# One stage instead of two: a layer's input products and its linear attention in a transformer kernel

## The reference, cut to what matters

```python
z = split_columns((rmsnorm(x, pre_g) * (1 + scale) + shift) @ w_in)
# pool branch: windowed means, a 128x128 product per group, a gate
y_pool = einsum('blgi,gio->blgo', multiscale_pool(z['pool_x']), pool_w) * pool_scale * silu(z['pool_gate'])
# GLA: decays, then a scan over chunks of 64 tokens, forwards and backwards
log_a = log_sigmoid(z['gla_af'] @ af_w2 + af_b) / 16        # and the same for gla_ab
y_gla = rmsnorm(scan_f + flip(scan_b), g) * silu(z['gla_gate'])
merged = sum(sigmoid(z['merge_b']) * (y_b @ w_branch_b) for b in (mla, pool, gla))   # 3 x 8 tiles of 128 columns
x = x + gate * rmsnorm(merged @ w_out, post_g)
```

## Time and profile before

| what | us |
|---|---|
| median of 3 runs | 1573.66 (1570.69 to 1574.66) |
| profiled execution | 1576.58 |
| its span in the trace | 1574.8 |
| PE busy in it | 1392.7 (88%) |
| mean granted TensorE clock | 0.946 of full speed |

### The profile page before, as it was taken

How to read it: one execution, slowest core, us unless ns; L and a number is a source line. 1 busy time by engine, 2 the same in 40 slices (tenths; PEclk the granted TensorE clock), 3 DMA queues, 4 the chain that set the end, 5 groups by cost and what they waited for, 6 DMA issues and landing times.

```text
span 1574.8 us, 24551 instructions
## 1 busy us (share of the span) xinstructions
PE 1392.7 (88%) x10288; PEld 1164.0 (74%) x10288; DVE 860.0 (55%) x1213; ACT 637.9 (41%) x1002; POOL 730.3 (46%) x512
## 2 busy tenths in 40 slices
PE   5898899999999999688889699979799888799996
PEld 1654588677777787373777689968688777799996
DVE  1566605351333340756687565659889635488811
ACT  2445332342322323446424464556422123565542
POOL 0520044323213554050494866747745204499983
PEclk8899999999999999899999899989899999999998
DMA  8320033244335432130333333525222123355552
GB/s 342 109 67 14 28 94 100 66 148 170 106 114 207 142 100 80 32 115 14 109 118 104 112 107 122 167 85 179 94 82 82 55 83 114 96 179 186 185 177 80
DMA packets 48830, 179.73 MB, mean 114 GB/s; under 512 B 5457, under 2 KB 6481, under 8 KB 48337
## 3 DMA queue, kind: packets, MB, share of 16 engines
q1 hardware_dynamic: 48576, 176.08, 34.3%
q10 hardware_dynamic: 144, 2.10, 0.3%
HBM read 177.11 MB, written 1.05 MB: 113 GB/s over the span
## 4 chain that ended last, share of the span: by engine, by line
PE 62%; DVE 22%; ACT 7%; DMA 3%; POOL 3%; issue 3%; ACTq 0%; DVEq 0%; SPq 0%
PE ps L367 16%; PE ps L371 15%; PE ps L368 15%; PE ps L369 15%; DMA panels<-weights 3%; DVE work L1776 2%; POOL panels_r L411 1%; POOL panels_r L412 1%; ACT panels_hi L401 1%; PE ps L879 1%; DVE work L1220 1%; DVE small L926 1%; DMA const_sb<-constants 1%; DVE work L1174 1%; DVE work L988 1%
## 5 line engine op out<-in xcount | busy, mean ns | idle before, releaser
L411 POOL TENSOR_TENSOR panels_r<-panels,panels_hi 128x512 fp32r<-128x512 f32 x254 | 368.5, 1451 | 823.5 <-ACT panels_hi L401 822.1
L368 PE MATMUL ps<-h_sb_r,panels_hi 128*128 128x256 f32 (+1 forms) x1408 | 455.3, 323 | 0.0
L401 ACT ACTIVATE panels_hi<-panels 128x1024 fp32r<-128x1024 f32 x254 | 267.2, 1056 | 420.6 <-PE ps L369 251.2
L412 POOL TENSOR_TENSOR panels_r<-panels,panels_hi 128x512 fp32r<-128x512 f32 x254 | 375.0, 1476 | 0.0
L367 PE MATMUL ps<-hi_sb_r,panels_hi 128*128 128x512 f32 (+1 forms) x784 | 280.3, 358 | 32.9 <-DVE h_sb_r L613 14.0
L368 PEld LDWEIGHTS ps<-h_sb_r,panels_hi 128*128 128x128 f32 x1408 | 278.4, 198 | 18.4 <-issue 1.2
L369 PE MATMUL ps<-hi_sb_r,panels_r 128*128 128x512 f32 (+1 forms) x784 | 274.6, 350 | 0.0
L367 PEld LDWEIGHTS ps<-hi_sb_r,panels_hi 128*128 128x128 f32 x784 | 154.8, 197 | 58.6 <-DVE h_sb_r L613 15.3
L367 PE MATMUL ps<-h_sb_r,panels_hi 128*128 128x256 f32 x624 | 184.6, 296 | 12.3 <-DVE h_sb_r L594 7.6
L367 PE MATMUL ps<-work_r,panels_hi 128*128 128x256 f32 (+1 forms) x560 | 183.1, 327 | 11.5 <-POOL panels_r L412 7.4
L369 PE MATMUL ps<-h_sb_r,panels_r 128*128 128x256 f32 x624 | 180.4, 289 | 0.0
(11 more groups left out here) (321 smaller groups left out, 1825.1 us busy)
## 6 DMA issues: line engine op xcount, KB each, us to landing
panels<-weights SPq DMA_DIRECT2D x326, 512.0 KB, 3.5
x_sb<-x_in SPq DMA_DIRECT2D x1, 2048.0 KB, 8.3
x_sb<-x_in ACTq DMA_DIRECT2D x1, 2048.0 KB, 8.7
const_sb<-constants SPq DMA_DIRECT2D x1, 1216.0 KB, 10.8
out<-x_sb SPq DMA_DIRECT2D x2, 512.0 KB, 2.9
vec_sb<-vectors SPq DMA_DIRECT2D x1, 725.0 KB, 12.1
small<-c_in SPq DMA_DIRECT2D x1, 8.0 KB, 1.6
```

The lines of the kernel that those rows point to most:

```text
L368: pe.matmul(o, lhsT.hi, rhs.lo, start=False, stop=False)
L401: act.activation(panels_hi[:, m:m + PANEL * P], panels[:, n:n + PANEL * P], ACT.Copy).then_inc(panel_rounded, 1)
L411: pool.tensor_tensor(panels_r[:, at:at + half], panels[:, at:at + half], panels_hi[:, m:m + half], ALU.subtract)
L412: pool.tensor_tensor(panels_r[:, at + half:at + 2 * half], panels[:, at + half:at + 2 * half], panels_hi[:, m + half:m + 2 * half], ALU.su ...
```

## The change

The two stages become one. The decay products now stand behind the tiles and in front of the values, in banks 4 to 7, so that none waits for a bank; ACT's absolute values and DVE's minima follow there, the minima into an area of their own (`la_first`). The values move to banks 1, 2, 3, 0 and the pool mixing behind them to banks 2, 0, 1, 3, so that the merge items can follow at once in banks 4 to 7. ACT's exponential and logarithm come behind the values, and DVE mixes items 0 and 1 between its scans (layer 1; item 0 in layer 0). In layer 1 step 2 of the table moves to an earlier place, behind tile 3, and each later step but the last one place forward; step 6 stands behind the minima. The four decay blocks move in the stream: they no longer share a panel with the pool blocks, so each layer has one panel more (328 for 326), which is the one in front of the values.

```diff
+        add(f"gla_w{l}", ...)          # now in front of gla_v, was behind pool_w
...
-   ("vector", 1): s5_factors, ("vector", 3): s5_turns(0, 2), ("vector", 9): s5_turns(2, 3),
-   ("vector", 10): s5_turns(3, 4), ("vector", 11): s5_turns(4, 5)} if last else {})
-            inputs = stages.pop()
+   ("vector", 1): s5_factors, ("vector", 3): s5_turns(0, 3), ("vector", 9): s5_turns(3, 4),
+   ("vector", 10): s5_turns(4, 5), ("vector", 11): s5_turns(5, 6)} if last else {})
+            head = stages.pop()
+            v_banks, mix_banks = (1, 2, 3, 0), (2, 0, 1, 3)
...
+            def pool_products(pe):
+                for g in range(4):
+                    pe.wait_ge(windowed, wd0 + g + 1)
+                    if g < 2:
+                        pe.wait_ge(v_act, va0 + g + 1)
+                    else:
+                        pe.wait_ge(v_dve, vd0 + g - 1)
+                    blocks.product(pe, ps[:, mix_banks[g], 0:TQ], blocks.lhs(pe, plan[f"pool_w{l}"] + g),
+                                   pooled[:, g, :, :].rearrange("p s t -> p (s t)"), True, True, mix_filled)
...
+            def decay_banks_free(pe):
+                pe.wait_ge(*by_dve)
+                pe.wait_ge(by_act[0], by_act[1] - 1)
...
-            stages.append(Stage(inputs_tensor, inputs_scalar, inputs_vector, None))
...
             def items(pe, first, end):
                     if i >= 2:
                         pe.wait_ge(mixed, m0 + i - 1)
+                    else:
+                        pe.wait_ge(w_min, wm0 + 2 * i + 2)
...
             def decay_products(pe):
+                inputs.decay_banks_free(pe)
                 for i in range(4):
-                    if i == 3:
-                        pe.wait_ge(w_min, wm0 + 1)
-                    blocks.product(pe, ps[:, i % 3, 0:TOK], ...)
+                    blocks.product(pe, ps[:, 4 + i, 0:TOK], ...)
...
             def decay_vector(dve):
-                for i in range(4):
-                    dve.wait_ge(w_abs, wa0 + i + 1)
-                    dve.tensor_scalar(la[...], ps[:, i % 3, 0:TOK], decay_bias(i), 0.0, ALU.add, ALU.min)...
                 dve.wait_ge(soft_done, so0 + 1)
                 dve.wait_ge(w_min, wm0 + 4)
-                step(dve.tensor_tensor(la, la, soft, ALU.subtract))
+                step(dve.tensor_tensor(la, la_first, soft, ALU.subtract))
                 for i in range(4):
                     step(dve.tensor_tensor_scan(su[:, i, :], ...))
+                    if i < 3:
+                        mixes(dve, i, min(i + 1, MIXES[l][0]))
...
             def tensor(pe):
+                inputs.head.tensor(pe)
                 decay_products(pe)
+                inputs.value_products(pe)
+                inputs.pool_products(pe)
                 items(pe, 0, cut[0])
...
             def scalar(act):
+                inputs.head.scalar(act)
                 round_y(act, 0)
-                decay_scalar(act)
+                decay_sizes(act)
+                inputs.values_scalar(act)
+                decay_logs(act)
                 gates(act, 0, GATES[l][0])
...
             def vector(dve):
                 steps["dve"](dve.memset(attn, 0.0))
+                inputs.head.vector(dve)
+                decay_minima(dve)
+                if inputs.turns is not None:
+                    inputs.turns(6, 7)(dve)
                 split_y(dve, 0)
+                inputs.values_vector(dve)
+                inputs.pools_vector(dve)
                 decay_vector(dve)
-                mixes(dve, 0, MIXES[l][0])
+                mixes(dve, 3, MIXES[l][0])
```

More of the change, by code:

```diff
@@ L141, in stream_plan @@
         add(f"gla_in{l}", z("gla_q") + z("gla_k") + a + z("gla_gate"), split=True)
+        add(f"gla_w{l}", [[part("gla_af_w2", l, 0, 16, m * P, P)] for m in range(2)]
+            + [[part("gla_ab_w2", l, 0, 16, m * P, P, 16)] for m in range(2)])
         add(f"gla_v{l}", [[part("w_in", l, k * P, P, IN_AT["gla_v"] + n * P, P)] for k in range(KD) for n in range(4)],
@@ L1027, in inputs_tensor, with values_scalar @@
                         w = blocks.lhs(pe, b0 + 4 * k, (0, P), 4)
-                        blocks.product(pe, ps[:, 1 + tt, :], h_split[:, k, tt * P:(tt + 1) * P], w, k == 0, k == KD - 1,
+                        blocks.product(pe, ps[:, v_banks[tt], :], h_split[:, k, tt * P:(tt + 1) * P], w, k == 0, k == KD - 1,
                                        v_filled if k == KD - 1 else None)
                 blocks.mark("gla_v", l)
[L1031 to L1040, removed]
+            def values_scalar(act):
                 rounding.before(act, "gla_v", l)
@@ L1043, in inputs_scalar, with values_vector @@
                     act.wait_ge(v_filled, vf0 + tt + 1)
[L1044 to L1049, removed]
+                    act.activation(gv[:, tt, :], ps[:, v_banks[tt], :], ACT.Copy).then_inc(v_act, 1)
+            def values_vector(dve):
                 for tt in (0, 2):
                     dve.wait_ge(v_filled, vf0 + tt + 1)
-                    dve.tensor_copy(gv[:, tt, :], ps[:, 1 + tt, :])
-                dve.wait_ge(*by_act)
+                    dve.tensor_copy(gv[:, tt, :], ps[:, v_banks[tt], :]).then_inc(v_dve, 1)
@@ L1061, in trunk @@
+            merged_split, merged_ready, linear = gla_and_merge(l, TQ, (y_mla, y_pool, y_gla), gq_at, (gq, gk, gv), ga, free_at,
+                                                               inputs)
             at = free_at
@@ L1093, in gla_and_merge @@
                 lent, hi0 = Room(x_sb), o_at
-                attn, states = lent(2, 2 * nt, P), lent(2, NCH, P)
+                attn = lent(2, 2 * nt, P)
+                la_first = region(x_sb, lent.at, 4, TOK)
+                states = lent(2, NCH, P)
             else:
@@ L1097, in gla_and_merge @@
                 low(4, TQ)
-                attn, states = low(2, 2 * nt, P), low(2, NCH, P)
+                attn = low(2, 2 * nt, P)
+                la_first = region(work, low.at, 4, TOK)
+                states = low(2, NCH, P)
             ys_at = gq_at - 3 * 4 * TQ
@@ L1197, in decay_products, with decay_sizes, decay_logs @@
             def decay_products(pe):
+                inputs.decay_banks_free(pe)
                 for i in range(4):
[L1199 to L1203 removed]
+                    blocks.product(pe, ps[:, 4 + i, 0:TOK], blocks.lhs(pe, plan[f"gla_w{l}"] + i), ga, True, True, w_filled)
+            def decay_sizes(act):
                 for i in range(4):
                     act.wait_ge(w_filled, w0 + i + 1)
[L1206 removed]
+                    act.activation(soft[:, row_of[i], :], ps[:, 4 + i, 0:TOK], ACT.Abs, bias=decay_bias(i)).then_inc(w_abs, 1)
+            def decay_logs(act):
                 act.wait_ge(w_abs, wa0 + 4)
```

25 lines of the change are left out of this document (16 added, 9 removed).

## The result

| | before | with the change |
|---|---|---|
| median, 19 runs each, us | 1574.66 | 1562.94 |
| ratio, 95% interval | 1 | 0.9931 [0.9916, 0.9947] |
| profiled execution, us | 1576.58 | 1558.46 |

A second comparison, with 10 runs of the change and 24 of before, gave 0.9953 [0.9930, 0.9975].

The account below looks back on a forecast made before the run. PE, busy 88% of the span, was taken as the bound, through its idle gaps and the low clock behind them. Layer 0's −5.1 and layer 1's −3.9 gave −9.0: 1573.66 to 1564.7 us, range 1558 to 1573.

Parts of the forecast that it names:

- Layer 0, −5.1: Layer 0: stage boundary −0.9, bank wait before the fourth decay product −2.5, low clock −1.7, together −5.1 us.
- rival (b): Panels keep their time: layer 0's gain lost at item 2's panel, layer 1 gains 2.5 us; 1571.2, chance 0.16.
- Layer 1, the tiles, +3.3: Before tiles 10 to 12: new gaps of 1.5, 1.2, 1.2 us, POOL alternating with DVE steps, less 0.58: +3.3.
- Rival (d): POOL keeps its lead, the tiles of layer 1 lose nothing: −3.3 us more, 1561.4; chance 0.13.
- (a): Clock stays low through tile 10 of layer 1: +3.0 us, 1567.7; chance 0.15.
- (c): Half clock from tile 9 to the end of tile 12 in layer 1: +13.9 us, 1578.6; chance 0.06.
- From the tiles to item 0: Layer 1: boundary −0.6, pool product wait −0.9, decay products at full clock −1.7 us; DVE about 1 us in hand.
- From item 0 to the scores, −4.0 − 1.7 + 1.7: Layer 1: 6.0 us of waiting instead of 10.0 (−4.0), low clock behind it gone (−1.7), one new fall (+1.7).
- The sum: Whole kernel: layer 0's −5.1 and layer 1's −3.9 give −9.0 us, put on the median.

Follow-up runs that it names:

- e11: The kernel before with a bank of its own for each of the four decay products: 0.9977 of before; layer 0 up to item 2 142.0 us, where before took 145.9.
- e1: The changed kernel with the table's steps back in their old places: 0.9919 of before; layer 1 up to the scores 136.8 us.
- e5: The changed kernel with each table step as two half instructions, same places: 0.9916 of before; layer 1 up to the scores 136.5 us.
- e6: The kernel before with only the mixes of items 0 and 1 moved between the scans: 0.9989 of before; layer 1 up to the scores 139.6 us.
- e8: The changed kernel with layer 1's mix of item 2 moved inside the exponents: 0.9917 of before; layer 1 up to the scores 136.3 us.
- e12: The changed kernel with item 2's mix inside the exponents, table steps in old places, item 2's first panel rounded before the logarithm: 0.9902 of before, median 1557.63 us.
- e4: The changed kernel with decay products, sizes and minima behind values and pools, as before: 0.9992 of before; layer 1 up to the scores 142.9 us.

## Why the prediction was right, point by point

**Layer 0, −5.1.** Measured −5.3 in A, in both profiles of the change. The three terms hold: no wait on the boundary, none on a bank, and by e11 the clock stays up once the bank wait is gone. e11 separates them: bank and clock 3.9, which leaves 1.4. Of this 0.89 is the boundary, and 0.4 the wait in front of item 2, 1.16 in e11 and 0.79 here. Item 2's panel moved with PE, 0.79 us of wait in front of it (0.73 before); rival (b) is out for layer 0.

**Layer 1, the tiles, +3.3.** Measured 1.46 + 0.95 + 0.94 − 0.58 = +2.8, at the places named, and e1 gives 3.0 for undoing it. The second and third waits were 0.95 and not 1.2. The panels came when I had them, one each 6.66 us (788.48 to 795.14); but PE's 24 products of a tile last 5.7 us up to the end of the last, where I had set 5.44, so less of the time shows as a wait. The alternation on which the term rests is shown by e5. Rival (d) is out.

**Rivals (a) and (c), the clock in the tiles.** Out: 0.54 in tile 9, 1.00 in tile 10, across a wait of 1.46; tile 9 was at 0.50 until 786.2, and the rise came in its last 0.8 us, while PE was busy. What the Trainium skill says (TensorE: Matmul & The Clock Gate, What's actually happening), that activity releases the throttle, agrees with these rows.

**From the tiles to item 0.** The new wait was 0.35, as forecast. DVE was 2.95 us early at the values, where I had given it 1: the windows took 21.8 us and not 26.9. POOL stood idle beside 5.1 us of them and beside 3.3 before; that this is the whole cause is not shown. The minima took 2.73 us for four while POOL worked, and POOL's halves took their 1.29 beside them:

```profile
829.87 1.29 POOL L412 TENSOR_TENSOR panels_r<-panels,panels_hi 128x512 fp32r<-128x512 f32 x1 [2.75 <-ACT panels_hi L402]
830.04 2.73 DVE L1234 TENSOR_SCALAR work<-ps,vec_sb 128x512 f32<-128x512 f32 x4
831.12 1.29 POOL L413 TENSOR_TENSOR panels_r<-panels,panels_hi 128x512 fp32r<-128x512 f32 x1
```

So what the Trainium skill says of DVE instructions with at most one SBUF input (SBUF — State Buffer, Who interferes with whom) fits.

**From item 0 to the scores, −4.0 − 1.7 + 1.7.** The waits were 1.92, 1.11 and 2.62, together 5.65 where I had 6.0. The sum fits better than its terms. I had 1.4 and 1.0 for the two panels behind item 2's first, and 1.11 was measured for both. I had 1.7 in front of item 4 and measured 2.62, because I took the exponents at the 5.9 us that they had before. They took 8.6, from 862.42 to 871.04, with POOL's halves beside them: the two small instructions above took 1.18 and 1.19 and not 0.17. I had priced the turns for POOL's halves and not for DVE's short instructions. And the clock fell behind two of the waits, 7.4 × 0.23 and 6.5 × 0.26, 1.7 us each, where I had taken one. That is why layer 1 gave 2.7 and not 3.9; e5 and e6 show that the second fall needn't have come.

Rival (b) is not out for layer 1 by the number alone. It had the time from DVE's subtraction to the scores unchanged at 30.3 us and 2.5 of gain. Measured are 30.3 (851.40 to 881.73) and 2.7. But its mechanism, a chain of fixed length, is out: that time is 27.6 in e8 and 25.4 in e12. That it came out the same in the change is a coincidence of a shorter wait, longer exponents and a second fall of the clock.

**The sum.** −5.3 − 2.7 = −8.0 from the traces, −9.0 forecast, −10.9 and −7.4 by the ratios. −9.0 lies in both intervals; −8.0 lies in the second and 0.3 us outside the first. A ends at item 2, and 0.4 to 0.6 us more are gained just behind it, where two waits for panels come to 2.2 and 2.1 us in the two profiles and to 2.8 before. So the forecast was right in its terms up to item 0 of both layers. In the last part of layer 1, errors of 1 to 2 us stood against each other in part, and that they came to only 1.2 is luck in part.

What the prediction did not see: that in layer 1 at least half of the gain was to be had by the mixes alone (e6), and that what the early decays gave there, 3.1 (e4), was eaten by the steps moved forward, 3.0 (e1).

## What to carry to other kernels

When a long wait is taken away, look at once for the second in line. Here the wait of 10.0 us was worth 1.5 to 2.8 as long as the next mix stood behind the exponents, and moving that one instruction gave 2 to 3.5 more. A step moved to fill an engine's idle time must be priced by what it does to the engine that takes turns with it: DVE had time in front of tile 8, POOL did not. A bound made of two engines in turn is counted in time per turn, not in turns, and for both engines: it was DVE's shortest instructions that lost most by it. And before a difference of 1 or 2 us is put down to an edit, see whether it already stands ahead of the place that the edit touches.

## What the runs showed of the hardware

The clock behind a short wait is not the same from one execution to the next. Both rows are the change, the same 76 products behind a wait of 1.77 us and one of 1.78; the first is from its first profile, the second from the other:

```profile
360.40:371.30 10.90, 10.89 (x76) 8.03 (x76) 2.29 (x7) 3.87 (x10) 1.93 (x2) 1.00 0.18 53
```

```profile
359.70:373.70 14.00, 13.97 (x76) 10.24 (x76) 2.30 (x7) 3.88 (x10) 1.76 (x2) 0.76 0.16 41
```

That is 3.1 us in one place, out of the spread of 13 to 16 us among single runs of one kernel. The wait in front of item 4 in layer 1 is a second such place (1.5 us, rows above). Whether the other places make up the rest was not tried.

DVE and POOL took turns here instruction by instruction, and both sides paid: a POOL half of 1.27 us takes 5.46 beside whole steps and 3.3 beside half steps, and a DVE instruction of 0.17 us takes 1.18 beside POOL's halves. DVE's minima, which read PSUM and one operand, took 2.73 us for four beside POOL's halves of 1.29, so neither lost time.
